# Joining the softmax parts of a dilated attention by exchanged log-sums, before the norm, in a two-layer decoder kernel

## Chip, core and metric

One core of one Trainium2 chip. The metric is device time of one execution of the whole kernel in microseconds (us), the median of several runs. The profile comes from one execution.

## What is computed

A decoder trunk on x (512 tokens, 1024 channels, f32): an RWKV-7 layer, a SwiGLU feed-forward, a dilated attention layer, a second feed-forward. The change is in the attention. Its core in the reference, for each of three groups (window, dilation) = (128, 1), (512, 4), (2048, 16):

```
q = rms_norm(qkv[:, :, g, 0], q_gain[g]) * scale      # 16 heads of 64
k = rms_norm(qkv[:, :, g, 1], k_gain[g])
logits = einsum(q_block, k_band) + bias               # keys t - j*dilation, banded
lse    = logsumexp(logits)
out_g  = exp(logits - lse) @ v
...
weights = softmax(stack(lse_g), axis=0)
o = sum_g(weights_g * out_g)
y = o.reshape(B, S, 1024) @ w_o
```

The kernel takes the three groups as two softmax parts: the near part (group 0, blocks of 128 neighbouring tokens with the block before), and the far part (groups 1 and 2 in one row of logits, tokens sorted by residue modulo 4).

## The kernel before

Everything lies transposed (channels on partitions, tokens along the free dimension). Weights come as 512 KB panels through two raw slots. A panel is split into a high and a low fp32r part, by ScalarE (`split_high`, line 1290) and VectorE (`split_low`, line 1722), two panels ahead of its use. A `product` is three fp32r matmuls of 128x512 for each of eight weight blocks; one output tile is 24 such matmuls.

The attention layer runs over eight head pairs. A pass `it` of the loop makes the nine tiles of pair `it` (query, key, value of three groups, i = 0 to 8) and weaves in the attention of the pair before, a = it - 1, in an order written out by hand for each engine:
- `projection_aux`: sum of squares of a query or key tile into bank 4 by two matmuls; ScalarE's Ln (1605) and Exp (1607) make the norm, VectorE applies it (2109, 2112). For a value tile, four transposes into bank 4 and a copy (1609). Squares are split by ScalarE and POOL first (1592, 1596, 2344).
- `logits`: four steps a pair (0 and 1 near, 2 and 3 far) into bank 2 + h for head h, at tiles 0 to 3. VectorE adds the bias and takes the maximum (2126), and negates it (2135).
- `exps` (1618, Ln at 1623) after tiles 2 and 4; `normalize` scales the probabilities by the inverse sums of their own part (2141 to 2152).
- `flip_probs`: transposes of probabilities (line 579) into bank 5, four groups for each head, at tiles 3 to 6, copied by ScalarE (1631); `attend` multiplies values with them at tiles 4 to 7, near into bank 6, far into bank 7.
- `lse_difference` at tile 7: 16 products with 128 columns into bank 4, which spread the difference of the log-sums over all tokens; sigmoid on ScalarE (1644, with two table loads); `combine` on VectorE (2160 to 2165): near - far, times the sigmoid, plus far; then copy and subtraction make the high and low parts of the result (1635, 2169).

Nearly all matmuls go through one helper at line 576, the transposes through 579. `fill_att` makes TensorE wait until a bank's use before was read, `att_read` makes an engine wait until it has been. SP issues the panels and, for each pair, the bias rows (line 565). `last_pair` weaves the attention of the eighth pair into the first tiles of the output projection (`heads(m, chunk)`, each three matmuls; chunk c needs the result of pair c).

## Time and profile before

| | |
|---|---|
| median of 3 runs | 1822.44 us (1822.4 to 1822.57) |
| profiled execution | 1821.82 us, its span 1820.0 us |
| TensorE busy | 1792.6 us, 98% |
| VectorE, ScalarE, POOL busy | 874.5, 768.8, 197.1 us |
| HBM | 89 GB/s over the span |

Busy times of TensorE are modelled ends and overlap, so starts are the better measure. An engine that is idle off the chain that ended last costs nothing.

### The profile page before, as it was taken

How to read it: one execution, taken by the hardware profiler on the slowest of the kernel's cores; microseconds unless marked ns; L12 is line 12 of the kernel's file. 1: busy time of each engine (PE TensorE's matmuls, PEld its weight loads, DVE VectorE, ACT ScalarE, POOL GpSimd, SP SyncE). 2: the span in 40 equal slices, each digit the busy share in tenths (PEclk: the TensorE clock that was granted, in tenths of full speed). 3: DMA queues.
4: the chain of work that ended last, by engine and by line, in shares of the span. 5: the costliest groups of instructions: out<-in, count | busy, mean ns of one | idle time of the engine just before them, and what ended most of it. 6: DMA issues, size and time to landing. Idle time of an engine off the chain costs nothing.

```text
span 1820.0 us, 36178 instructions
## 1 busy us (share of the span) xinstructions
PE 1792.6 (98%) x15618; PEld 1368.7 (75%) x15618; DVE 874.5 (48%) x1517; ACT 768.8 (42%) x1308; POOL 197.1 (11%) x172
## 2 busy tenths in 40 slices
PE   8999999999999999999999999999999999999999
PEld 3746666666478888888887887887887788888887
DVE  5824444454364444333455555555555544444322
ACT  6434444442252232222556656656657532323221
POOL 0033334432100000000111111111110000000000
PEclk9999999999999999999999999999999999999999
DMA  3321212121123323333232222222222123223332
GB/s 125 103 69 51 82 67 67 64 98 53 59 93 98 99 93 94 103 100 98 93 93 70 82 82 70 81 82 70 81 83 70 62 94 100 93 94 103 100 98 93
DMA packets 57541, 155.00 MB, mean 85 GB/s; under 512 B 5591, under 2 KB 22535, under 8 KB 57384
## 3 DMA queue, kind: packets, MB, share of 16 engines
q1 hardware_dynamic: 57288, 152.63, 26.0%
q8 instruction: 124, 2.03, 0.5%
q14 instruction: 33, 0.27, 0.0%
q10 hardware_dynamic: 96, 0.07, 0.0%
HBM read 150.51 MB, written 11.61 MB: 89 GB/s over the span
## 4 chain that ended last, share of the span: by engine, by line
PE 92%; ACT 4%; DVE 2%; issue 1%; DMA 1%; POOL 1%; ACTq 0%; DVEq 0%; POOLq 0%
PE bank L576 89%; PE bank L579 3%; ACT f L1618 2%; DVE f L2152 0%; DVE r L2024 0%; ACT f L1605 0%; ACT f L1631 0%; ACT r L1290 0%; ACT r L1596 0%; DMA f<-const 0%; DMA f<-stream 0%; ACT f L1592 0%; DVE r L1722 0%; DVE f L1733 0%; DVE f L1769 0%
## 5 line engine op out<-in xcount | busy, mean ns | idle before, releaser
L576 PE MATMUL bank<-r 128*128 128x512 f32 x5424 | 1255.6, 391 | 2.3 <-DVE r L2024 1.0
L576 PEld LDWEIGHTS bank<-r 128*128 128x128 f32 x5424 | 1012.0, 188 | 225.3 <-issue 10.8
L576 PE MATMUL bank<-f 64*64 64x64 f32 (+5 forms) x9762 | 503.5, 255 | 16.5 <-ACT f L1315 4.2
L1722 DVE TENSOR_TENSOR r<-f,r 128x1024 fp32r<-128x1024 f32 x222 | 274.8, 1238 | 392.4 <-ACT r L1290 392.4
L576 PEld LDWEIGHTS bank<-f 64*64 64x64 f32 (+3 forms) x9762 | 308.7, 140 | 200.6 <-issue 133.1
L1290 ACT ACTIVATE r<-f 128x1024 fp32r<-128x1024 f32 x222 | 232.5, 1048 | 147.4 <-PE bank L576 141.5
L2344 POOL TENSOR_TENSOR r<-f,r 128x512 fp32r<-128x512 f32 x48 | 62.2, 1295 | 839.1 <-ACT r L1596 839.1
L1575 ACT ACTIVATE r<-f 128x512 fp32r<-128x512 f32 x44 | 27.8, 632 | 215.6 <-DVE f L2063 215.6
L2093 DVE TENSOR_TENSOR f<-bank,f 128x512 f32<-128x512 f32 x72 | 56.2, 780 | 73.4 <-PE bank L576 70.1
L1572 ACT ACTIVATE f<-f 128x512 f32<-128x512 f32 x44 | 27.8, 632 | 110.5 <-DVE f L2053 110.5
L1605 ACT ACTIVATE f<-bank,f 128x512 f32<-128x512 f32 x48 | 32.9, 686 | 94.9 <-PE bank L576 94.9
L579 PE MATMUL bank<-f 128*128 128x128 f32 x432 | 63.9, 277 | 5.4 <-DVE f L2152 4.3
L2057 DVE TENSOR_TENSOR f<-bank,f 128x512 f32<-128x512 f32 x44 | 30.4, 691 | 76.5 <-PE bank L576 76.5
L1631 ACT ACTIVATE f<-bank 128x512 f32<-128x512 f32 (+1 forms) x64 | 36.2, 566 | 71.6 <-PE bank L579 71.4
L579 PEld LDWEIGHTS bank<-f 128*128 128x128 f32 x432 | 49.3, 140 | 21.9 <-ACT f L1631 7.8
L1618 ACT ACTIVATE f<-f 128x256 f32<-128x256 f32 (+1 forms) x128 | 61.4, 482 | 2.6 <-DVE f L2135 2.6
L1448 ACT ACTIVATE f<-bank 128x512 f32<-128x512 f32 (+1 forms) x40 | 23.8, 596 | 78.3 <-PE bank L576 78.3
L2109 DVE SCALAR_TENSOR_TENSOR f<-f 128x512 f32<-128x512 f32 x32 | 37.0, 1155 | 30.0 <-ACT f L1607 30.0
L1860 DVE TENSOR_TENSOR f<-bank,f 128x512 f32<-128x512 f32 x40 | 27.7, 691 | 46.9 <-PE bank L576 46.9
L1867 DVE COPY f<-bank 128x512 f32<-128x512 f32 (+1 forms) x40 | 27.7, 692 | 46.1 <-PE bank L576 46.0
L2053 DVE TENSOR_TENSOR f<-bank,f 128x512 f32<-128x512 f32 x44 | 30.4, 691 | 32.4 <-PE bank L576 27.4
L2126 DVE CUSTOM_DVE_ANT_0 f<-bank,f 128x256 f32<-128x256 f32 (+1 forms) x128 | 44.4, 402 | 1.9 <-PE bank L576 1.1
(109 smaller groups left out, 919.4 us busy)
## 6 DMA issues: line engine op xcount, KB each, us to landing
f<-stream SPq DMA_DIRECT2D x246, 512.0 KB, 3.5
bias_copies<-bias_rows SPq DMA_DIRECT2D x6, 1536.0 KB
f<-xT SPq DMA_DIRECT2D x16, 256.0 KB, 4.6
f<-lora_out SPq DMA_DIRECT2D x16, 128.0 KB, 6.4
f<-bias_copies SPq DMA_DIRECT2D x16, 128.0 KB, 3.2
f<-bias_copies SPq DMA_DIRECT2D x32, 64.0 KB, 2.9
outT<-f SPq DMA_DIRECT2D x8, 256.0 KB, 4.3
f<-const SPq DMA_DIRECT2D x1, 576.0 KB, 3.7
```

The lines of the kernel that those rows point to most:

```text
L576: return nc.tensor.matmul(out, lhsT, rhs, start=start, stop=stop, skip_group_check=True)
L579: return nc.tensor.transpose(out, in_, con(C_ID))
L1290: A(r(hi_at(q), 1024), f(O_RAW + p % RAW * 1024, 1024), ACT.Copy)\
L1605: free(A(f(O_QS), banks[4][:, :], ACT.Ln, bias=kol(K_EPS), scale=1.0 / HD), 4)
L1618: A(tile, tile, ACT.Exp, bias=f(sm + 8 + n, 1), accum_out=f(sm + 16 + n, 1))\
L1631: free(A(f(O_PT + n % N_PT * S, w), banks[5][:, 0:w], ACT.Copy), 5)
L1722: TT(r(lo_at(q), 1024), f(O_RAW + panel_of(q) % RAW * 1024, 1024), rf(hi_at(q), 1024), ALU.subtract).then_inc(s["w_lo"], 1)
L2053: TT(f(O_FT + i % 2 * S), bank_of(t)[:, :], f(O_RSTD), ALU.mult)\
L2093: TT(out, in0, in1, ALU.mult).then_inc(freed(t), 1)
L2109: STT(by_residue(to), bc(f(O_QR + n % 2 * S), (4, P), (1, 4)), gain, bc(f(O_QS), (4, P), (1, 4)), ALU.mult, ALU.mult).then_inc(s["qk_norm" ...
L2126: ins = V.tensor_tensor_reduce(out=f(O_P + h * 4 * S + n * 2 * P + first, w), in0=banks[b][:, e * 2 * P + first:(e + 1) * 2 * P], in1=f(O_ ...
L2344: TT(r(O_QL), f(O_QQ), rf(O_QH), ALU.subtract).then_inc(s["q_sq_lo"], 1)
```

## The change

- The near queries are written so that inside a block of 128 tokens they are sorted by residue modulo 4 (VectorE norm in four pieces), and the near bias rows come in the same order: four DMAs of 32 partitions in place of one, for each head.
- `exchange_lse` replaces `lse_difference`: right after tile 5, four products with a 128x128 selection matrix and 16 columns bring each row the log-sums of the other part. VectorE picks them, subtracts its own and clips (`other_lse`), ScalarE takes one Exp (`weights`), VectorE makes 1 / (own sum * (1 + exp(difference))) (`scales`). The probabilities are scaled with this (`normalize`), so both parts add up in bank 6 and nothing is combined afterwards. The far attends write bank 6 in four runs of 32 columns.
- `logits` runs two steps at tile 1 and two at tile 3, even ones into banks 2 and 3, odd ones into 5 and 7. On ScalarE the exponentials stand ahead of the norm of tiles 1 and 3.
- Transposes go to bank 5 for head 0 and 7 for head 1, both heads together, at tiles 6, 7, 8 and tile 0 of the next pass; attends at tile 8 and tile 1 of the next pass.
- `last_pair` has a new order. Near the kernel's start one small constant (4 columns) is loaded more, on which the first bias product waits.

The diff, cut to its core (removed code can be read in the kernel above):

```diff
--- before.py
+++ after.py
@@ -396,23 +397,24 @@
+        def logits_bank(h, pair):
+            return 5 + 2 * h if pair % 2 else 2 + h
...
         def att_step(b, name, hp):
             if b in (2, 3):
...
+                return 2 * hp + name[1] // 2
+            if b in (5, 7):
+                return 6 * hp + (name + 2 if isinstance(name, int) else name[1] // 2)
...
             if name == "lse":
-                return base(hp + 1) + (8 if hp < NHP - 1 else 1)
+                return base(hp + 1) + (6 if hp < NHP - 1 else 1)
...
-            return base(hp) + (name + 1 + (name == 7) if hp else name)
+            return base(hp) + (name + 1 + (name >= 5) if hp else name)
...
@@ -502,6 +504,7 @@
+                    sp.dma_start(f(O_SM + 80, 4), const[:, C_QUARTER:C_QUARTER + 4]).then_inc(s["oh_in"], 16)
@@ -557,8 +560,14 @@
                     if hp:
-                        att_read(sp, 2 + h, (h, 3), hp - 1)
-                    for g, at, width in ((0, 0, 2 * P), (1, 2 * P, P), (2, 3 * P, P)):
+                        for pair in (2, 3):
+                            att_read(sp, logits_bank(h, pair), (h, pair), hp - 1)
+                    for c in range(4):
+                        src = bass.AP(tensor=bias_copies.tensor, offset=(2 * hp + h) * P * 384 + P - 1 + 383 * c,
+                                      ap=[[4 * 383, 32], [1, 2 * P]])
+                        sp.dma_start(f(O_BIAS + h * S, 2 * P, 32 * c, 32 * c + 32), src).then_inc(s[f"bias_in{h}"], 16)
+                    for g, at, width in ((1, 2 * P, P), (2, 3 * P, P)):
@@ -1134,7 +1143,7 @@
                         for h in range(2):
-                            o = banks[2 + h][:, e * 2 * P:(e + 1) * 2 * P]
+                            o = banks[logits_bank(h, pair)][:, e * 2 * P:(e + 1) * 2 * P]
...
@@ -1148,44 +1157,42 @@
+            def flip_probs(hp, g):
+                for h in range(2):
+                    b = 5 + 2 * h
+                    fill_att(b, g, hp)
+                    pe.wait_ge(s[f"probs{h}"], 8 * hp + (4 if g < 2 else 8))
+                    for j, what in enumerate(GROUPS[g]):
+                        last = flip(banks[b][:, j * P:(j + 1) * P], f(block_of(h, what), P))
+                    last.then_inc(s["flipped"], 1)
             def attend(hp, g):
                 for h in range(2):
...
+                    att_read(pe, 5 + 2 * h, g, hp)
+                if g == 0:
+                    if hp:
+                        pe.wait_ge(s["att_lo"], hp)
+                    att_read(pe, 4, 2, hp)
                 if g == 2:
                     att_read(pe, 4, 8, hp)
-                if g == 0:
-                    att_read(pe, 4, 2, hp)
                 for j, (kind, q, e) in enumerate(GROUPS[g]):
...
+                    v = O_VT + hp % 2 * 3 * S + (q - 1 + e) * P if kind == "A" else O_VT + (hp % 2 * 3 + 1 + e) * S + q * P
                     for h in range(2):
                         lo, n = HD * h, flip_turn(hp, h, g)
-                        last = mm(banks[b][lo:lo + HD, q * P:(q + 1) * P], f(v + lo, HD),
-                                  f(O_PT + n % N_PT * S + j * P, P), g in (0, 2) and j == 0, False)
+                        o = banks[6][lo:lo + HD, :].rearrange("p (n c j) -> p n c j", n=4, c=4)
+                        last = mm(o[:, q, :, :] if kind == "A" else o[:, :, q, :], f(v + lo, HD),
+                                  f(O_PT + n % N_PT * S + j * P, P), g == j == 0, False)
                 last.then_inc(s["attended"], 1)
-            def lse_difference(hp):
+            def exchange_lse(hp):
                 fill_att(4, "lse", hp)
...
+                pe.wait_ge(s["lse"], hp + 1)
+                if hp == 0:
+                    pe.wait_ge(s["quarters"], 1)
+                for c in range(4):
+                    last = mm(banks[4][:, 16 * c:16 * (c + 1)], f(O_E4 + c * P, P), bc(f(O_SM + 32, 48), (40, 2), (1, 8)))
                 last.then_inc(s["lse_ps"], 1)
...
             for it in range(NHP):
...
                 for i in range(9):
...
@@ -1206,16 +1213,22 @@
                     if i == 0:
                         projection_aux(a, 8)
...
+                    if i == 0 and b >= 0:
+                        flip_probs(b, 3)
+                    if i in (1, 3):
+                        logits(a, i - 1)
                         logits(a, i)
...
+                    if i == 1 and b >= 0:
+                        attend(b, 2)
+                        attend(b, 3)
+                    if i == 5:
+                        exchange_lse(a)
+                    if i in (6, 7):
+                        flip_probs(a, i - 6)
+                    if i == 8:
+                        attend(a, 0)
+                        attend(a, 1)
+                        flip_probs(a, 2)
             def last_pair(a):
@@ -1225,38 +1238,36 @@
                 heads(0, 0)
                 projection_aux(a, 8)
+                flip_probs(a - 1, 3)
                 logits(a, 0)
+                attend(a - 1, 2)
                 heads(0, 1, 2)
+                attend(a - 1, 3)
                 logits(a, 1)
...
                 logits(a, 3)
...
+                heads(1, 1, 2, 3, 4, 5)
+                heads(2, 0, 1, 2, 3, 4)
+                exchange_lse(a)
+                heads(2, 5)
+                heads(3, 0, 1, 2, 3)
+                flip_probs(a, 0)
+                heads(3, 4)
+                flip_probs(a, 1)
+                heads(3, 5)
                 attend(a, 0)
...
+                flip_probs(a, 2)
+                heads(0, 6)
                 attend(a, 1)
...
+                flip_probs(a, 3)
                 attend(a, 2)
-                flip_probs(a, 1, 3)
-                heads(2, 4, 5)
+                heads(1, 6)
                 attend(a, 3)
...
+                heads(2, 6)
+                heads(3, 6)
                 for m in range(4):
                     heads(m, KC - 1)
@@ -1597,6 +1608,8 @@
             def projection_aux(hp, i):
...
+                if kind == 2 and hp >= 2:
+                    act.wait_ge(s["attended"], 4 * (hp - 2) + (4 if g else 2))
                 act.wait_ge(s["aux_ps"], 9 * hp + i + 1)
@@ -1627,78 +1640,62 @@
-                w = len(GROUPS[g]) * P
-                free(A(f(O_PT + n % N_PT * S, w), banks[5][:, 0:w], ACT.Copy), 5)
+                w, b = len(GROUPS[g]) * P, 5 + 2 * h
+                free(A(f(O_PT + n % N_PT * S, w), banks[b][:, 0:w], ACT.Copy), b)
+            def weights(hp):
+                act.wait_ge(s["ex_step"], 7 * hp + 6)
+                A(f(O_EX + 112, 16), f(O_EX + 112, 16), ACT.Exp).then_inc(s["ex_exp"], 1)
             def combine(hp):
-                att_read(act, 7, None, hp)
-                A(r(O_O + hp * S), f(O_DF), ACT.Copy).then_inc(s["att_hi"], 1)
+                act.wait_ge(s["attended"], 4 * (hp + 1))
+                A(r(O_O + hp * S).rearrange("p (n j c) -> p n j c", n=4, c=4),
+                  banks[6][:, :].rearrange("p (n c j) -> p n j c", n=4, c=4), ACT.Copy).then_inc(s["att_hi"], 1)
...
+            def keep_both(a, g):
+                for h in range(2):
+                    keep_flipped(a, h, g)
             for it in range(NHP):
...
                 for i in range(9):
...
+                    split_high(p_of(T_QKV + 9 * it + i) + LEAD)
+                    if a >= 0 and i in (2, 4):
+                        for h in range(2):
+                            exps(a, h, i // 2 - 1)
                     if i:
                         projection_aux(it, i - 1)
-                    if a >= 0 and 3 <= i <= 6:
-                        keep_flipped(a, 1, i - 3)
+                    elif a >= 0:
+                        projection_aux(a, 8)
+                    if i == 0 and b >= 0:
+                        keep_both(b, 3)
+                    if a >= 0 and i in (6, 7):
+                        keep_both(a, i - 6)
...
+                    if i == 2 and b >= 0:
+                        combine(b)
+                    if i == 5:
+                        weights(a)
+                    if i == 8:
+                        keep_both(a, 2)
             def last_pair(a):
                 projection_aux(a, 8)
+                keep_both(a - 1, 3)
                 split_high(PAN_WO1 + 3)
+                combine(a - 1)
                 exps(a, 0, 0)
                 exps(a, 1, 0)
                 split_high(PAN_WO1 + 4)
-                keep_flipped(a, 0, 0)
                 exps(a, 0, 1)
-                keep_flipped(a, 1, 0)
                 exps(a, 1, 1)
...
+                weights(a)
+                for g in range(4):
+                    keep_both(a, g)
                 combine(a)
...
@@ -2102,21 +2099,28 @@
+                        for h in range(2):
+                            dve.wait_ge(s[f"logits{h}"], 4 * (hp - 1))
...
+                    elif kind == 0:
+                        for c in range(4):
+                            part = lambda off: bc(f(off + c, S - 3), (P, 4), (4, 32))
+                            last = STT(bc(f(to + 32 * c, S - 96), (P, 4), (1, 32)), part(O_QR + n % 2 * S), gain,
+                                       part(O_QS), ALU.mult, ALU.mult)
+                        last.then_inc(s["qk_norm"], 1)
@@ -2131,68 +2135,91 @@
             def negate_max(hp, h, half):
...
-                att_read(dve, 2 + h, (h, 2 * half + 1), hp)
+                for pair in (2 * half, 2 * half + 1):
+                    att_read(dve, logits_bank(h, pair), (h, pair), hp)
                 TS(f(sm + 8, 4), f(sm, 4), -1.0, None, ALU.mult).then_inc(s[f"neg_max{h}"], 1)
+            def both_heads(off, n=8):
+                return bc(f(off, 40 + n), (40, 2), (1, n))
+            def total(hp):
+                for h in range(2):
+                    dve.wait_ge(s[f"log{h}"], 2 * hp + 2)
+                TT(both_heads(O_SM + 32), both_heads(O_SM + 32), both_heads(O_SM), ALU.add).then_inc(s["lse"], 1)
+            def other_lse(hp):
+                def step(ins, n):
+                    ins.then_inc(s["ex_step"], 1)
+                    dve.wait_ge(s["ex_step"], 7 * hp + n)
+                dve.wait_ge(s["lse_ps"], hp + 1)
+                att_free(TT(bc(f(O_EX, 64), (4, 16), (1, 4)), banks[4][:, 0:64].rearrange("p (u n) -> p u n", n=4),
+                            bc(f(O_SM + 80, 4), (0, 16), (1, 4)), ALU.mult), 4)
+                att_read(dve, 4, "lse", hp)
+                step(TT(bc(f(O_EX + 64, 32), (2, 16), (1, 2)), bc(f(O_EX, 62), (4, 16), (1, 2)),
+                        bc(f(O_EX + 2, 62), (4, 16), (1, 2)), ALU.add), 1)
+                step(TT(f(O_EX + 96, 16), bc(f(O_EX + 64, 31), (2, 16)), bc(f(O_EX + 65, 31), (2, 16)), ALU.add), 2)
+                for half in range(2):
+                    step(TT(bc(f(O_EX + 112 + 4 * half, 12), (8, 2), (1, 4)),
+                            bc(f(O_EX + 96 + 1 - half, 15), (2, 2), (4, 4)),
+                            both_heads(O_SM + 32 + 4 * half, 4), ALU.subtract), 3 + half)
+                step(TS(f(O_EX + 112, 16), f(O_EX + 112, 16), 80.0, None, ALU.min), 5)
+                TS(f(O_EX + 112, 16), f(O_EX + 112, 16), -80.0, None, ALU.max).then_inc(s["ex_step"], 1)
+            def scales(hp):
+                dve.wait_ge(s["ex_exp"], hp + 1)
+                STT(both_heads(O_SM + 24), bc(f(O_EX + 112, 16), (8, 2), (1, 8)), kol(K_ONE), both_heads(O_SM + 16),
+                    ALU.add, ALU.mult).then_inc(s["ex_step"], 1)
+                dve.wait_ge(s["ex_step"], 7 * hp + 7)
+                V.reciprocal(both_heads(O_SM + 24), both_heads(O_SM + 24)).then_inc(s["inv_sum"], 1)
             def normalize(hp, h, half):
...
+                dve.wait_ge(s["inv_sum"], hp + 1)
                 for n in range(4):
                     first = P if n == half == 0 else 0
                     tile = f(O_P + h * 4 * S + (4 * half + n) * 2 * P + first, 2 * P - first)
                     TS(tile, tile, f(sm + 24 + n, 1), None, ALU.mult).then_inc(s[f"probs{h}"], 1)
...
             def combine_low(hp):
+                natural = lambda ap: ap.rearrange("p (n j c) -> p n j c", n=4, c=4)
                 dve.wait_ge(s["att_hi"], hp + 1)
-                TT(r(O_O + (KC + hp) * S), f(O_DF), rf(O_O + hp * S), ALU.subtract).then_inc(s["att_lo"], 1)
+                TT(natural(r(O_O + (KC + hp) * S)), banks[6][:, :].rearrange("p (n c j) -> p n j c", n=4, c=4),
+                   natural(rf(O_O + hp * S)), ALU.subtract).then_inc(s["att_lo"], 1)
...
+            V.tensor_copy(bc(f(O_E4), (P, 4), (32, 4), (1, 32)), bc(con(C_ID), (32, 4), (0, 4), (1, 32)))\
+                .then_inc(s["quarters"], 1)
...
             for it in range(NHP):
...
                 for i in range(9):
+                    if a >= 0 and i == 5:
+                        total(a)
...
+                    if i in (1, 3):
                         for h in range(2):
+                            biased(a, h, i - 1)
                             biased(a, h, i)
...
+                            negate_max(a, h, i // 2)
+                    if i == 3 and b >= 0:
+                        combine_low(b)
+                    if i == 5:
+                        other_lse(a)
+                        scales(a)
+                    if i in (5, 6):
                         for h in range(2):
-                            normalize(a, h, i // 2 - 1)
+                            normalize(a, h, i - 5)
             def last_pair(a):
@@ -2206,18 +2233,18 @@
                 negate_max(a, 0, 0)
                 negate_max(a, 1, 0)
                 split_low(PAN_WO1 + 3)
+                combine_low(a - 1)
                 both(2)
-                normalize(a, 0, 0)
                 both(3)
                 negate_max(a, 0, 1)
                 negate_max(a, 1, 1)
...
                 split_low(PAN_WO1 + 4)
...
+                total(a)
+                other_lse(a)
+                scales(a)
+                for half in range(2):
+                    for h in range(2):
+                        normalize(a, h, half)
                 combine_low(a)
...
```

## Rows read from the trace of the kernel before

**Rows 1.** The page: busy time of each engine, and the chain that ended last.
```profile
PE 1792.6 (98%) x15618; PEld 1368.7 (75%) x15618; DVE 874.5 (48%) x1517; ACT 768.8 (42%) x1308; POOL 197.1 (11%) x172
...
PE 92%; ACT 4%; DVE 2%; issue 1%; DMA 1%; POOL 1%; ACTq 0%; DVEq 0%; POOLq 0%
```

**Rows 2.** Windows, one pass: length, busy us (count) of PE, PEld, DVE, ACT, POOL, clock.
```profile
1059.50:1127.90 68.40, 67.77 (x413) 55.01 (x412) 37.46 (x89) 41.94 (x85) 7.77 (x6) 1.00 0.24 79
```

**Rows 3.** Waits of TensorE, 923 to 1401 us (total, times, longest).
```profile
PE bank L579 <- DVE f L2152: 4.3, 7, 0.6
```

**Rows 4.** Timeline of TensorE in one pass: start, length, what, how many.
```profile
1066.43 1.13 PE L576 MATMUL bank<-f 64*128 64x256 f32 x8
...
1080.29 1.03 PE L579 MATMUL bank<-f 128*128 128x128 f32 x8
1081.25 1.16 PE L576 MATMUL bank<-f 64*128 64x128 f32 x16
1082.35 0.65 PE L579 MATMUL bank<-f 128*128 128x128 f32 x4
1082.76 6.19 PE L576 MATMUL bank<-r 128*128 128x512 f32 x26
1088.78 0.49 PE L579 MATMUL bank<-f 128*128 128x128 f32 x3
1089.20 1.09 PE L576 MATMUL bank<-f 128*64 128x128 f32 x16
1090.22 0.55 PE L579 MATMUL bank<-f 128*128 128x128 f32 x3
...
1098.59 0.63 PE L579 MATMUL bank<-f 128*128 128x128 f32 x4 [0.63 <-DVE f L2152]
...
1113.04 2.84 PE L576 MATMUL bank<-f 128*64 128x128 f32 x48
1115.81 11.63 PE L576 MATMUL bank<-r 128*128 128x512 f32 x50
1127.28 0.60 PE L579 MATMUL bank<-f 128*128 128x128 f32 x4
```

**Rows 5.** The last of 26 stream matmuls, then ScalarE's timeline after it.
```profile
1066.12 0.39 PE L576 MATMUL bank<-r 128*128 128x512 f32 x1
...
1066.54 0.69 ACT L1605 ACTIVATE f<-bank,f 128x512 f32<-128x512 f32 x1 [3.06 <-PE bank L576]
1067.26 0.63 ACT L1607 ACTIVATE f<-f 128x512 f32<-128x512 f32 x1
```

**Rows 6.** Timeline of VectorE: combining, small steps, norm by residue, scaling.
```profile
1059.73 0.68 DVE L2160 TENSOR_TENSOR f<-f,bank 128x512 f32<-128x512 f32 x1
1060.44 0.69 DVE L2163 TENSOR_TENSOR f<-f 128x512 f32<-128x512 f32 x1
...
1069.97 0.64 DVE L2135 TENSOR_SCALAR f<-f 128x4 f32<-128x4 f32 x2
...
1079.41 0.18 DVE L2141 RECIPROCAL f<-f 128x4 f32<-128x4 f32 x1 [0.71 <-ACT f L1618]
...
1097.31 1.14 DVE L2152 TENSOR_SCALAR f<-f 128x256 f32<-128x256 f32 x4
...
1114.53 1.15 DVE L2109 SCALAR_TENSOR_TENSOR f<-f 128x512 f32<-128x512 f32 x1 [1.14 <-ACT f L1607]
```

**Rows 7.** Bias loads on SP: min/median/max ns of one issue.
```profile
L565 SPq DMA_DIRECT2D f<-bias_copies x48: 319/432/1643, 885.8 to 1362.1; - x48
```

**Rows 8.** Timeline of TensorE in the last pair: first small piece, the two waits, the end.
```profile
1396.25 0.63 PE L579 MATMUL bank<-f 128*128 128x128 f32 x4
...
1411.34 0.55 PE L579 MATMUL bank<-f 128*128 128x128 f32 x3 [0.21 <-ACT f L1631]
...
1416.31 0.66 PE L579 MATMUL bank<-f 128*128 128x128 f32 x4 [0.77 <-ACT f L1631]
...
1424.80 11.41 PE L576 MATMUL bank<-r 128*128 128x512 f32 x49
```

More of the change, by code:

```diff
@@ L80 @@
 C_OH = C_RESET + 512
-N_CONST = C_OH + 3 * 384
+C_QUARTER = C_OH + 3 * 384
+N_CONST = C_QUARTER + 4
 def shape_constants():
@@ L214 @@
 O_BIAS = O_VR + S
-O_OA = O_BIAS + 2 * S
-O_DF = O_OA + S
-O_DW = O_DF + S
-assert O_DW + S <= O_B
+O_EX = O_BIAS + 2 * S
+O_E4 = O_EX + S
+assert O_E4 + S <= O_B
 O_O = O_HD
@@ L1128, in logits @@
                 for h in range(2):
-                    fill_att(2 + h, (h, pair), hp)
+                    fill_att(logits_bank(h, pair), (h, pair), hp)
                 pe.wait_ge(s["qk_norm"], 6 * hp + (2 if pair < 2 else 6))
@@ L1149, in block_of @@
                 return O_P + h * 4 * S + (n + (4 if kind == "B" else 0)) * 2 * P + e * P
-            def flip_probs(hp, h, g):
-                fill_att(5, (h, g), hp)
-                pe.wait_ge(s[f"probs{h}"], 8 * hp + (4 if g < 2 else 8))
-                for j, what in enumerate(GROUPS[g]):
-                    last = flip(banks[5][:, j * P:(j + 1) * P], f(block_of(h, what), P))
-                last.then_inc(s["flipped"], 1)
+            def flip_probs(hp, g):
[6 more added lines that the diff above has]
+                    last.then_inc(s["flipped"], 1)
@@ L1158, in attend @@
             def attend(hp, g):
                 for h in range(2):
-                    att_read(pe, 5, (h, g), hp)
-                if g in (0, 2):
-                    fill_att(6 if g == 0 else 7, None, hp)
+                    att_read(pe, 5 + 2 * h, g, hp)
[3 more added lines that the diff above has]
+                    att_read(pe, 4, 2, hp)
                 if g == 2:
                     att_read(pe, 4, 8, hp)
-                if g == 0:
-                    att_read(pe, 4, 2, hp)
@@ L1176, in attend @@
                 last.then_inc(s["attended"], 1)
-            def lse_difference(hp):
+            def exchange_lse(hp):
                 fill_att(4, "lse", hp)
-                for h in range(2):
-                    pe.wait_ge(s[f"lse{h}"], 2 * (hp + 1))
-                for n in range(2 * NT):
-                    for h in range(2):
-                        lo = HD * h
-                        o = banks[4][lo:lo + HD, n * P:(n + 1) * P] if n < NT else \
-                            banks[4][lo:lo + HD, n - NT:S:4]
-                        last = mm(o, bc(f(O_SM + 40 * h + 32 + n, 1), (0, HD)), con(C_ID), n == 0, False)
+                pe.wait_ge(s["lse"], hp + 1)
[3 more added lines that the diff above has]
+                    last = mm(banks[4][:, 16 * c:16 * (c + 1)], f(O_E4 + c * P, P), bc(f(O_SM + 32, 48), (40, 2), (1, 8)))
@@ L1195, in _ @@
             for it in range(NHP):
-                a = it - 1
+                a, b = it - 1, it - 2
                 for i in range(9):
@@ L1662, in _ @@
                     if i:
                         projection_aux(it, i - 1)
-                    if a >= 0 and 3 <= i <= 6:
-                        keep_flipped(a, 1, i - 3)
+                    elif a >= 0:
[4 more added lines that the diff above has]
+                        keep_both(a, i - 6)
                     squares(it, i)
@@ L2115, in biased @@
             def biased(hp, h, pair):
-                b = 2 + h
+                b = logits_bank(h, pair)
                 dve.wait_ge(s[f"logits{h}"], 4 * hp + pair + 1)
-                dve.wait_ge(s[f"bias_in{h}"], 48 * (hp + 1))
+                dve.wait_ge(s[f"bias_in{h}"], 96 * (hp + 1))
                 if hp:
@@ L2137, in normalize @@
+            def scales(hp):
[4 more added lines that the diff above has]
+                V.reciprocal(both_heads(O_SM + 24), both_heads(O_SM + 24)).then_inc(s["inv_sum"], 1)
             def normalize(hp, h, half):
                 sm = O_SM + 40 * h + 4 * half
-                dve.wait_ge(s[f"exp{h}"], 8 * hp + 4 * half + 4)
@@ L2141, in normalize @@
-                V.reciprocal(f(sm + 24, 4), f(sm + 16, 4)).then_inc(s["inv_sum"], 1)
-                inv = 4 * hp + 2 * half + h + 1
-                dve.wait_ge(s[f"log{h}"], 2 * hp + half + 1)
-                if half:
-                    TT(f(sm + 32, 4), f(sm + 8, 4), f(sm + 32, 4), ALU.subtract).then_inc(s[f"lse{h}"], 1)
-                else:
-                    TT(f(sm + 32, 4), f(sm, 4), f(sm + 32, 4), ALU.add).then_inc(s[f"lse{h}"], 1)
-                dve.wait_ge(s["inv_sum"], inv)
+                dve.wait_ge(s["inv_sum"], hp + 1)
@@ L2182, in _ @@
                         continue
-                    if i == 0 and a:
-                        combine(a - 1)
-                    if i < 4:
+                    if i in (1, 3):
                         for h in range(2):
+                            biased(a, h, i - 1)
                             biased(a, h, i)
-                        if i % 2:
-                            for h in range(2):
-                                negate_max(a, h, i // 2)
-                    if i == 0 and a:
-                        combine_low(a - 1)
-                    if i in (2, 4):
+                            negate_max(a, h, i // 2)
[5 more added lines that the diff above has]
+                    if i in (5, 6):
                         for h in range(2):
-                            normalize(a, h, i // 2 - 1)
+                            normalize(a, h, i - 5)
             def last_pair(a):
```

98 lines of the change are left out of this document (4 added, 94 removed).

## The prediction

> **What bounds the kernel now.** I read the page first: TensorE is busy 98% of the span and the chain that ended last is 92% TensorE [rows 1]. So only what TensorE executes, or waits for, can move the time. Next the windows: one pass of the attention loop (nine projection tiles of one head pair, with the attention of the pair before woven in) is 68.4 us long [rows 2], seven such passes follow each other, and the last pair is woven into the output projection. Its clock stays at 1.00, so nothing of the clock enters the sum. In the list of waits TensorE waits in the seven passes for one thing, a VectorE scaling of probabilities, 0.6 us each time [rows 3]. ScalarE (41.9 us of 68.4) and VectorE (37.5) have room, but in places only.
>
> In the timeline of one pass [rows 4] I subtract starts from starts, since the printed ends overlap. The pass falls into eight pieces of the 228 stream matmuls (the products, and the sums of squares made with them), 53.0 us, and eight pieces of small work, the first at 1066.43 and the last at 1127.28: 1.07, 1.10, 2.47, 1.75, 2.41, 2.40, 2.77 and 1.38 us, together 15.35. That is 68.35, the whole pass. I price the parts from the same rows. Sixteen attend matmuls alone take 1.02, sixteen with 32 log-sum matmuls 2.77: so 0.0547 each, 1.75 for the log-sums, and about 0.145 for leaving such a piece. Eight transposes before an attend piece take 0.96, three 0.42: 0.108 each and 0.1 for the change; four before the stream take 0.41 (1082.35 to 1082.76), no extra. Logits of one step: 1.38 less four transposes, 0.53, is 0.85 for the first, then 1.07, 1.10 and 1.10 (1081.25 to 1082.35), each with some 0.1 for leaving. An unbroken piece of 50 stream matmuls takes 11.47 (1115.81 to 1127.28), one of 26 takes 6.02 (1082.76 to 1088.78): 24 more are 5.45, 0.227 each, so 26 should be 5.90 and a break costs 0.12.
>
> **The change on TensorE, per pass.** After it, small work stands in seven places:
> - tile 0: 4 transposes of the value tile and 8 of probabilities: 1.25
> - tile 1: two logits steps and 32 attend matmuls: 0.85 + 1.07 - 0.1 + 1.75 + 0.145 = 3.7
> - tile 3: 4 value transposes, two logits steps: 0.52 + 1.10 + 1.10 - 0.1 = 2.6
> - tile 5: the exchange, and a new wait (below)
> - tile 6: 12 transposes 1.25; tile 7: 6 transposes 0.6; tile 8: 28 attend matmuls and 8 transposes, 1.68 + 0.85 = 2.5.
>
> The exchange is 4 products with 16 columns, thus 8 instructions (each f32 product is two: the 8 products of the first attend group stand as 16). No row has 16 columns on full weights. From below: 128 columns take 0.109, so 16 take 0.014, 0.1 in all. From above: each as long as a whole transpose, 0.109, 0.9 in all. I take 0.6, nearer the upper end, since the weights to be loaded are the transposes' own size; with leaving the piece 0.7.
>
> **The new wait.** The exchange writes bank 4, directly after the sums of squares of tile 4 were put there. It must wait until ScalarE's Ln of line 1605 has read them. Before, 16 attends stood between. Ln starts 0.42 us after the start of the last of those matmuls and takes 0.69 [rows 5]; TensorE resumes 0.14 after a releaser's end (the scalings from 1097.31 end at 1098.45, it starts at 1098.59) [rows 4, 6]. It would have gone on 0.31 after that start (1066.12 to 1066.43). So 0.42 + 0.69 + 0.14 - 0.31 = 0.94, say 0.93 us of wait per pass. Behind it on TensorE stand the next product and everything after.
>
> Sum of small work: 1.25 + 3.7 + 2.6 + 0.7 + 0.93 + 1.25 + 0.6 + 2.5 = 13.5. The old wait is already within the 15.35. Stream: one break less, 0.1. Net per pass 15.35 - 13.5 + 0.1 = 1.95; I take 1.9, for mode changes (logits to attends) that no row shows side by side. Seven passes: 13.3.
>
> **Does the long chain fit?** The exchange must now reach the probabilities before the first transposes, one tile later. Count from the end of tile 4's sums: Ln and Exp end at 1.4, VectorE's norm by residue (1.15) at 2.6 [rows 5, 6]. Behind it on VectorE are the exchange's seven steps. A small one lasts 0.18, and a dependent one starts 0.03 after the end before it (1060.41 to 1060.44) [rows 6]: with the wider first one 1.4, to 4.0. ScalarE's Exp of 16 columns, taken as about as short, 0.25; addition and reciprocal 0.4: 4.7. Scaling four blocks takes 1.07 per head: 5.8 and 6.9. TensorE gets there after wait 0.8, exchange 0.7, product 5.6 and value transposes 0.45: 7.65, and 8.2 for the second head. So the cover is there, with 1.3 to 1.8 us left, and the old wait of 0.6 goes and nothing takes its place in tile 6. What is queued behind ScalarE's wait for VectorE (`weights`) is the split of a weight panel two tiles ahead: some 3 us later, used 8 us later. The next nearest: ScalarE's two copies of transposes (0.6 each) stand ahead of the squares of tile 7; POOL then needs 1.3, and I find 1.0 us left before TensorE asks for them.
>
> **Moved or removed beside TensorE, costed at nothing.** VectorE's three combining steps and ScalarE's near copy, sigmoid and two table loads go [rows 5, 6]. The exponentials (4 x 0.5 us and a Ln for each head, 4.5 a half) now stand ahead of Ln/Exp of tiles 1 and 3 on ScalarE: by my count they end 1.1 us before tile 1's sums and 0.15 after tile 3's, which have a whole tile until anybody needs them. VectorE's query norm of the first group becomes four pieces (0.75 to about 1.2), logits use it a pass later. SP issues 12 instead of 6 bias loads per pair, at 0.43 each, 2.6 us more ahead of one weight panel [rows 7], and waits for the last biased bank about 1.5 us longer. A panel is split two tiles (14 us) before its use, which hides it. The extra small load at the start stands ahead of weight panels by one issue, 0 to 0.4 us.
>
> A rule of the Trainium skill (PSUM — Partial Sum Buffer, Specifications) speaks against the change: it says of the 8-byte cachelines that any non-contiguous access pattern "slows matmuls significantly", and the far groups now write bank 6 in four runs of 32 with gaps. The trace disagrees for a stricter pattern: half of the 32 log-sum matmuls write every fourth column, and all 48 together fit one price of 0.0547 us [rows 4].
>
> **The last pair.** Its small pieces take 14.05 us now (ten of them between 1396.25 and 1424.80) [rows 8]; built as above they are 15.1, since the previous pair's third and fourth attends and last transposes (2.6 us) come in and 1.05 of the log-sums goes. The two waits of 0.21 and 0.77 there and their slow restarts go: 1.1. New ones: 0.35 for the second head's probabilities, 0.1 for a bank, 0.1 to 0.2 at the end, where the joined result of the last pair now has two products (1.4 us) as cover for copy 0.65 and subtraction 0.69, instead of ten. Net 0.5 more. In exchange the first pass is without a pair behind it: 2.6 less.
>
> **Sum.** 13.3 + 2.6 - 0.5 = 15.4 us. The profiled execution took 1821.82 us (span 1820.0); the median of the runs is 0.6 above it. 1822.4 - 15.4 = 1807.0; I say 1807.2 with the start's load.
>
> **Rivals.**
> 1. The chain is late (slower side). If each of some nine dependent steps between exchange and scaling costs 0.57, near the 0.64 that two small negations behind a reduction take together [rows 6], instead of 0.2, the chain is 3.3 us longer. From 1.3 us on it decides; 2.0 us per pass come onto TensorE, 14, and some 3.3 in the last pair: 1824.5. Against it: those stand behind a reduction, the reciprocal and the subtraction of the combining do not and take 0.18 and 0.69 + 0.03. 7%.
> 2. The strided write costs. If the 32 far attends took double, 1.75 for eight pairs is 14: 1821.2. The Trainium skill's rule above would give this; the rows speak against. 7%, with everything else that would end within 0.2%.
> 3. The change doesn't do what its last words say: merging logits in four banks saves nothing, as new changes of shape cost what old ones did. Of the 1.9 per pass, 1.15 is the exchange, 0.8 the old wait, -0.93 the new; 0.9 is merging. Without it 6.3 less gain: 1813.5. 10%.
> 4. ScalarE's copies ahead of the squares hold TensorE at tile 7: if 2 us late instead of 1 early, 1 us per pass: 1814. 9%.
> 5. More than forecast: the exchange hides at the lower bound (0.5 x 8) and no mode change costs: 1802. 9%.
>
> The forecast has 58% (1804 to 1811). A measurement of this kernel can tell about 0.2% (3.6 us): faster by more 86%, within 7%, slower 7%. The range reaches over forecast and rivals 3 and 4, and a little of 5: 1803 to 1817.
>
> **What would show it.** Pass 66.4 us instead of 68.3. TensorE's wait for VectorE's scaling gone from the list of waits, one for Ln of line 1605's successor there with 0.9 us seven times, before a piece of 8 matmuls with 16 columns. That piece 0.3 to 0.9. A piece of 32 attends near 1.75 (double would be rival 2). If TensorE waits for the scaling in tile 6, rival 1; for POOL or the squares in tile 8, rival 4. The forecast is wrong if the pass is above 67.5 or below 65.5.

## The result and the profile after

The changed kernel took 1804.83 us, median of 4 runs (1803.7 to 1806.13), against 1822.51 for the kernel before on the same chip (1822.4 to 1826.07): ratio 0.9901, 95% interval 0.9886 to 0.9917. That is 17.7 us, or 1.0%, faster. The prediction said 1807.2, range 1803 to 1817, faster with 86%.

The profiled execution took 1806.13 us, its span is 1804.3, 15.7 less than the span before. The busy times on its page:

```profile
PE 1775.9 (98%) x15426; PEld 1362.0 (75%) x15426; DVE 881.7 (49%) x1534; ACT 741.6 (41%) x1285; POOL 198.4 (11%) x172
```

TensorE is still the bound, busy 98%, but with 192 instructions and 16.7 us of busy time less than in [rows 1]. The chain in order of time (start, length, what) shows where the time went:

```profile
520.83 366.81 PE bank L585 x1614
...
1023.53 0.69 ACT f L1618
...
1089.84 0.69 ACT f L1618
...
1445.69 355.45 PE bank L585 x1565
```

From the first of these rows (in the first feed-forward) to the last (the start of the second one's stream) is 924.86 us. The same chain of before has 520.30 for the first and 1461.37 for the last, 941.07 us: 16.2 less. Up to the first row the profile after is 0.5 later, and after the last both run 355.5. Where the first of the seven passes begins, it is still 0.5 later (923.50 against 922.99), so all of the gain lies in the attention layer. One pass, from Ln to Ln (line 1618 after, 1605 before), is 66.31 us, 1089.84 - 1023.53, instead of 68.35 (68.4 in the window of [rows 2]).

The timeline of TensorE over one pass, tile 0 to tile 8 (start, length, what, how many, idle time before and what ended it):

```profile
1052.77 1.47 PE L588 MATMUL bank<-f 128*128 128x128 f32 x12
1054.00 6.17 PE L585 MATMUL bank<-r 128*128 128x512 f32 x26
1060.10 3.69 PE L585 MATMUL bank<-f 64*128 64x128 f32 x48
1063.71 11.63 PE L585 MATMUL bank<-r 128*128 128x512 f32 x50
1075.18 0.60 PE L588 MATMUL bank<-f 128*128 128x128 f32 x4
1075.71 2.06 PE L585 MATMUL bank<-f 64*128 64x128 f32 x32
1077.70 12.10 PE L585 MATMUL bank<-r 128*128 128x512 f32 x52
1090.58 1.06 PE L585 MATMUL bank<-f 128*128 128x16 f32 x8 [0.78 <-ACT f L1618]
1091.49 5.73 PE L585 MATMUL bank<-r 128*128 128x512 f32 x24
1097.06 1.47 PE L588 MATMUL bank<-f 128*128 128x128 f32 x12
1098.29 6.18 PE L585 MATMUL bank<-r 128*128 128x512 f32 x26
1104.31 0.82 PE L588 MATMUL bank<-f 128*128 128x128 f32 x6
1104.88 6.17 PE L585 MATMUL bank<-r 128*128 128x512 f32 x26
1110.98 1.75 PE L585 MATMUL bank<-f 128*64 128x128 f32 x28
1112.66 1.09 PE L588 MATMUL bank<-f 128*128 128x128 f32 x8
1113.51 5.73 PE L585 MATMUL bank<-r 128*128 128x512 f32 x24
```

Seven pieces of small work, as forecast: from the start of each to the start of the stream behind it they take 1.23, 3.61, 2.52, 0.91 (the exchange), 1.23, 0.57 and 2.53 us, and the exchange is preceded by a wait. The list of TensorE's waits over the attention layer (total, times, longest), which answers to [rows 3]:

```profile
PE bank L585 <- ACT f L1618: 5.4, 7, 0.8
PE bank L588 <- DVE f L2186: 0.4, 1, 0.4
```

The wait for scaled probabilities in every pass is gone, and the one for ScalarE's Ln is there, seven times 0.78. Rival 1 would have shown line 2186 here seven times; it stands there once, in the last pair, where 0.35 was forecast. Rival 4 would have shown a wait for POOL or for the squares of tile 7, and none is in the list. VectorE's chain in the same pass:

```profile
1091.22 1.14 DVE L2107 SCALAR_TENSOR_TENSOR f<-f 128x512 f32<-128x512 f32 x1 [0.79 <-ACT f L1620]
1092.21 0.21 DVE L2158 TENSOR_TENSOR f<-bank,f 128x64 f32<-128x64 f32 x1
...
1093.96 0.23 DVE L2174 SCALAR_TENSOR_TENSOR f<-f 128x16 f32<-128x16 f32 x1 [0.28 <-ACT f L1648]
...
1094.51 2.06 DVE L2186 TENSOR_SCALAR f<-f 128x128 f32<-128x128 f32 x8
```

The exchange's steps start at 1092.21, after the norm of line 2107, and the probabilities of both heads are scaled at 1096.57. TensorE's first transposes of them come after the four of the value tile, at about 1097.5. Read from these rows, the chain fits with some 1.4 to 1.8 us left; the experiment with 13 more steps below finds 1.2.

### The profile page after: what moved, and what is told of

It reads as the page before. It is cut to its first block, busy times and chain, and to the rows that moved or that the text cites. A ratio compares the mean times of both kernels' runs of the same rounds, so it can differ in the third digit from the quotient of the medians.

```text
span 1804.3 us, 35872 instructions
## 1 busy us (share of the span) xinstructions
PE 1775.9 (98%) x15426; PEld 1362.0 (75%) x15426; DVE 881.7 (49%) x1534; ACT 741.6 (41%) x1285; POOL 198.4 (11%) x172
## 4 chain that ended last, share of the span: by engine, by line
PE 95%; DVE 2%; ACT 1%; issue 1%; DMA 1%; POOL 1%; SPq 0%; ACTq 0%; DVEq 0%; POOLq 0%
PE bank L585 92%; PE bank L588 3%; DVE r L2021 0%; ACT f L1618 0%; ACT r L1301 0%; DMA f<-xT 0%; DMA f<-const 0%; DMA f<-stream 0%; DVE r L1719 0%; DVE f L1730 0%; DVE f L1766 0%; DVE r L1775 0%; DVE f L2033 0%; DVE f L2186 0%; POOL f L2290 0%
## 5 line engine op out<-in xcount | busy, mean ns | idle before, releaser
L585 PE MATMUL bank<-f 64*64 64x64 f32 (+7 forms) x9570 | 490.4, 254 | 22.4 <-ACT f L1618 5.4
L1719 DVE TENSOR_TENSOR r<-f,r 128x1024 fp32r<-128x1024 f32 x222 | 280.3, 1263 | 376.5 <-ACT r L1301 376.5
L585 PEld LDWEIGHTS bank<-f 64*64 64x64 f32 (+3 forms) x9570 | 302.2, 140 | 205.9 <-issue 127.9
L588 PE MATMUL bank<-f 128*128 128x128 f32 x432 | 57.8, 275 | 0.4 <-DVE f L2186 0.4
L1459 ACT ACTIVATE f<-bank 128x512 f32<-128x512 f32 (+1 forms) x40 | 23.8, 596 | 77.9 <-PE bank L585 77.9
L2130 DVE CUSTOM_DVE_ANT_0 f<-bank,f 128x256 f32<-128x256 f32 (+1 forms) x128 | 44.9, 402 | 12.6 <-PE bank L585 11.7
L1622 ACT ACTIVATE f<-bank 128x512 f32<-128x512 f32 x24 | 14.3, 597 | 79.3 <-PE bank L588 79.3
```

The lines of the kernel that those rows point to most:

```text
L585: return nc.tensor.matmul(out, lhsT, rhs, start=start, stop=stop, skip_group_check=True)
L588: return nc.tensor.transpose(out, in_, con(C_ID))
L1719: TT(r(lo_at(q), 1024), f(O_RAW + panel_of(q) % RAW * 1024, 1024), rf(hi_at(q), 1024), ALU.subtract).then_inc(s["w_lo"], 1)
L2130: ins = V.tensor_tensor_reduce(out=f(O_P + h * 4 * S + n * 2 * P + first, w), in0=banks[b][:, e * 2 * P + first:(e + 1) * 2 * P], in1=f(O_ ...
```

## The experiments

In the following, "stretch" is the time between the two long TensorE pieces of the chain shown above (924.86 us after, 941.07 before). It is used because the time up to the first one differs between profiles of equal code: it is at 520.83 us in the profile after and at 515.62 in a second profile of the same kernel, whose stretch is 924.90. The readings of each version come from one profile of it.

### The new wait taken away: the exchange in another bank

```diff
+        def lse_bank(hp):
+            return 2 if hp < NHP - 1 else 4
...
-                    last = mm(banks[4][:, 16 * c:16 * (c + 1)], ...
+                    last = mm(bank[:, 16 * c:16 * (c + 1)], ...
```

(with the turns of banks 2 and 4, and VectorE's read, changed to match)

> The changed kernel with the exchange of the first seven pairs in bank 2, which is free by then, instead of bank 4; the last pair as it was. My theory: the 0.78 us in which TensorE waits for ScalarE's Ln of tile 4's sums is a pure loss, so the piece after the last sum starts 0.2 instead of 1.17 us after it, a pass takes 66.31 - 0.94 = 65.4 us and the span is 6.6 us shorter than the changed kernel's 1804.3. Rival: VectorE's chain from exchange to scaled probabilities is anchored at the same Ln, so TensorE only waits 0.9 us later, at the transposes of tile 6, and the pass stays at 66.3.

Stretch 917.67 us, 7.2 less; a pass 65.28. The exchange stands in the stream with no idle time ahead of it:

```profile
1082.71 0.96 PE L590 MATMUL bank<-f 128*128 128x16 f32 x8
1083.52 5.75 PE L590 MATMUL bank<-r 128*128 128x512 f32 x24
```

No wait for line 1618's Ln is left, and none came at the transposes. So the wait was a pure loss of 1.03 us a pass (0.94 expected): 0.78 idle and some 0.25 around it. Of these, 0.10 lie in the piece itself, which takes 0.81 without a pause ahead of it (1082.71 to 1083.52) instead of 0.91. The rival falls.

### Logits apart

```diff
-                    if i in (1, 3):
-                        logits(a, i - 1)
+                    if i < 4:
                         logits(a, i)
```

> The changed kernel with the four logits steps issued apart, at tiles 0, 1, 2 and 3, still in four banks; VectorE's order is unchanged. My theory: merging them saves changes of shape; apart, the pass has one break more in the stream and three more changes, 0.17 + 0.10 + 0.09 + 0.10 + 0.13 = 0.6 us, so 66.9 us a pass and 4.2 us in all. Rival (merging saves nothing, what changed is only which bank): the pass stays at 66.3.

Stretch 930.59 us, 5.7 more; a pass is 67.13, 0.82 more. The steps at tiles 0, 1 and 2 of such a pass:

```profile
1053.12 0.93 PE L585 MATMUL bank<-f 64*128 64x128 f32 x8
1053.98 6.19 PE L585 MATMUL bank<-r 128*128 128x512 f32 x26
1060.10 3.03 PE L585 MATMUL bank<-f 64*128 64x256 f32 x40
...
1069.17 1.16 PE L585 MATMUL bank<-f 64*128 64x128 f32 x16
```

The first step costs 0.86 here, and the stream is broken again at 1069.17. Merging is thus worth 0.82 us a pass, more than the 0.6 expected here, and rival 3 of the prediction (0.9 of the gain doesn't come) falls. Counting the changes of shape gives the right sign and about the size; it does not explain 0.2 of the 0.82.

### The far part written without gaps

```diff
-                        last = mm(o[:, q, :, :] if kind == "A" else o[:, :, q, :], f(v + lo, HD),
+                        last = mm(o[:, q, :, :], f(v + lo, HD),
```

> The changed kernel with the far attends written to 128 neighbouring columns of bank 6 instead of four runs of 32 (the parts are thus added in the wrong order of tokens; the work is the same). My theory: the write pattern costs nothing, pass and span stay within 0.3 us. Rival (the Trainium skill, PSUM — Partial Sum Buffer, Specifications: patterns that are not contiguous slow matmuls): the 32 far attends of a pair, 0.77 to 0.92 us a group of 16 now, get clearly shorter, up to 0.9 us a pass.

The output of this version is wrong, since its far parts land on the wrong tokens. Stretch 924.89 us, a difference of 0.03; the piece with 16 logits and 32 attend matmuls in it has the same length to 0.01 us:

```profile
1054.99 3.69 PE L585 MATMUL bank<-f 64*128 64x128 f32 x48
1058.61 5.73 PE L585 MATMUL bank<-r 128*128 128x512 f32 x24
```

TensorE's output in runs of 32 f32 columns with gaps costs nothing here. The sentence of the Trainium skill (PSUM — Partial Sum Buffer, Specifications) does not hold for this write, and rival 2 falls.

### The exponentials behind the norm

```diff
-                    if a >= 0 and i in (2, 4):
-                        for h in range(2):
-                            exps(a, h, i // 2 - 1)
                     if i:
                         projection_aux(it, i - 1)
...
                     squares(it, i)
                     if a < 0:
                         continue
+                    if i in (2, 4):
+                        for h in range(2):
+                            exps(a, h, i // 2 - 1)
```

> The changed kernel with ScalarE's exponentials behind the norm and the squares of their tile, as before the change. In the prediction I costed their place at nothing. Seen from the trace after, I now expect that it costs: the second half would run from about 1086.4 to 1091 instead of ending at 1083.8, so the Ln for which TensorE waits at the exchange starts about 2.2 us later, the wait grows from 0.8 to 3 us and a pass takes 68.5 us, the span 15 us more. Rival (place costs nothing): 66.3 a pass.

Stretch 960.11 us, 35 more than after and 19 more than before; the passes take 71.4 to 71.8, only the first 70.5. The direction was as expected, the size more than twice that: the waits are 3.3 to 3.6 us (2.7 in the first pass), against 3 expected, and what follows them is slow.

```profile
1171.83 1.89 PE L585 MATMUL bank<-f 128*128 128x16 f32 x8 [3.63 <-ACT f L1618]
1173.56 7.52 PE L585 MATMUL bank<-r 128*128 128x512 f32 x24
1180.92 1.47 PE L588 MATMUL bank<-f 128*128 128x128 f32 x12
```

The eight instructions take 1.73 us instead of 0.91, and the 24 of the stream 7.36 instead of 5.57 (1091.49 to 1097.06). That is 2.6 us, beside 2.85 of longer wait in this pass: 66.31 + 2.6 + 2.85 = 71.8. The windows (length, TensorE's busy time, granted clock, DMA share, GB/s) show why:

```profile
1154.00:1168.00 14.00, 14.00 (x86) 1.00 0.41 114
...
1171.80:1173.50 1.70, 1.67 (x8) 0.50 0.08 14
1173.50:1176.00 2.50, 2.50 (x8) 0.50 0.60 200
1176.00:1178.00 2.00, 2.00 (x8) 0.66 0.00 0
```

The granted clock is 1.00 before the pause and 0.50, the lower of its two levels (1.2 GHz), after it, until about 1177.4. So the place of the exponentials, which the prediction costed at nothing, is what makes the exchange right after tile 5 pay: they have to be out of ScalarE's way before the Ln that TensorE waits for.

### How much cover the chain has

```diff
+                for k in range(13):
+                    TS(f(O_EX + 112, 16), f(O_EX + 112, 16), -80.0, None, ALU.max).then_inc(s["pad"], 1)
+                    dve.wait_ge(s["pad"], KC + 13 * hp + k + 1)
```

> The changed kernel with 13 more dependent VectorE steps (a clip repeated, no change of values) between exchange and scaling: 13 x 0.21 = 2.7 us. In the trace after, the first head's scaling ends some 1.8 us and the second's 1.4 us ahead of its transposes. My theory (a cover, then microsecond for microsecond): TensorE comes to wait 1.0 for the first head and 0.5 more for the second in tile 6, pass 67.8 us; in the last pair, where nothing is left, 2.7: some 13 us in all. Rival 1 of the prediction (each step costs 0.57): 7.4 us more chain, 6 us a pass, 45 us. Rival (chain not on the path at all): 66.3 a pass.

Stretch 939.57 us, 14.7 more; a pass 67.83. VectorE's 13 steps and TensorE's transposes in one pass:

```profile
1093.56 2.69 DVE L2170 TENSOR_SCALAR f<-f 128x16 f32<-128x16 f32 x13
...
1098.52 0.63 PE L588 MATMUL bank<-f 128*128 128x128 f32 x4 [0.80 <-DVE f L2189]
1099.50 0.63 PE L588 MATMUL bank<-f 128*128 128x128 f32 x4 [0.36 <-DVE f L2189]
```

A dependent small step costs 0.21 us (2.69 / 13), not 0.57. The 2.7 us of delay come out as 1.52 a pass: so 1.2 us of it were covered, near the 1.3 that the prediction named as the point from which the chain decides. The mechanism of rival 1 is real, its price isn't. In the last pair the delay costs 4.0 us instead of 2.7. There the pause is 2.79 us, and the windows show the low clock after it, as above:

```profile
1413.70 0.83 PE L588 MATMUL bank<-f 128*128 128x128 f32 x4 [2.79 <-DVE f L2189]
...
1414.00:1416.00 2.00, 1.85 (x9) 0.50 0.00 0
1416.00:1418.00 2.00, 2.00 (x10) 0.65 0.00 0
```

### A pause between those

The same, with 19 steps.

> The changed kernel with 19 more dependent VectorE steps in the chain, 4.0 us. With 13 steps (2.7 us) TensorE waited 0.80 and 0.36 us and its clock stayed at 1.00; after a pause of 2.8 us in the last pair, and of 3.6 us with the exponentials last, the granted clock showed 0.50 for some microseconds. Theory A (only waits): a pause of 2.1 and one of 0.36, pass 67.83 + 1.27 = 69.1 us. Theory B (a pause of 2.1 us already brings the lower clock): the stream after it runs at half speed for some 2 to 4 us, pass 70 to 72 us, and the clock of the pass under 1.00.

Stretch 956.53 us. Six passes in order (length, TensorE busy, clock, DMA share, GB/s):

```profile
981.27:1051.97 70.70, 67.51 (x389) 0.98 0.25 75
1051.97:1121.06 69.09, 65.90 (x389) 1.00 0.25 77
1121.06:1191.73 70.67, 67.48 (x390) 0.98 0.25 75
1191.73:1260.79 69.06, 65.88 (x389) 1.00 0.26 77
1260.79:1329.86 69.07, 65.88 (x390) 1.00 0.26 77
1329.86:1400.54 70.68, 67.50 (x390) 0.98 0.25 75
```

Both theories hold in turn. With the same pause of 2.05 us in each of these six, the clock fell after it in three, which take 70.7, and stayed in three, which take 69.07, as theory A says to 0.1 us. The seventh such pause stands ahead of these windows, in the first pass (2.04 us, TensorE resumes at 963.40), and there the clock fell too: 0.50 from 964 to 966. So it fell after four of seven equal pauses, and cost 1.3 us in the first pass and 1.6 in the others. The last pair has a pause of 4.05 us, after which it fell as well. Why one pass and not the next is open.

### The width of the exchange

```diff
-                    last = mm(banks[4][:, 16 * c:16 * (c + 1)], f(O_E4 + c * P, P), bc(f(O_SM + 32, 48), (40, 2), (1, 8)))
+                    last = mm(banks[4][:, 64 * c:64 * (c + 1)], f(O_E4 + c * P, P), bc(f(O_SM + 32, 48), (0, 4), (40, 2), (1, 8)))
```

(with VectorE's read changed to match)

> The changed kernel with each of the four exchange products four times as wide (64 columns, the same sixteen repeated; VectorE reads the first sixteen). In the trace after the eight instructions follow each other every 0.112 us, which I had put at 0.6 for all and which is the price of a transpose with 128 columns. My theory: full 128x128 f32 weights set this price, not columns, so with 64 columns the piece still takes 0.91 us and a pass 66.3. Rival (a column price below 128, and a start of its own for each): the piece grows by 0.1 us or more.

Stretch 924.90 us, and the piece again 0.91 long:

```profile
1087.08 1.10 PE L585 MATMUL bank<-f 128*128 128x64 f32 x8 [0.78 <-ACT f L1618]
1087.99 5.73 PE L585 MATMUL bank<-r 128*128 128x512 f32 x24
```

Four times the columns cost nothing. So an f32 matmul on full weights costs the same at 16 and at 64 columns: 0.11 us here, behind a pause, and 0.10 in the last pair, where no pause stands ahead (8 in 0.80 us with 64 columns, in 0.81 with 16). Twelve transposes with 128 columns take 1.23 us, 0.10 each, too. That it is the load of the weights which sets this price is argued, not shown: the log-sum products had half the weights and cost half, 0.0547, with 128 columns, but no run changed the weights alone.

### The removed products by themselves

```diff
-                for n in range(2 * NT):
+                for n in range(2 * NT - 1, 2 * NT):
```

(with the output's columns changed to match)

> The kernel before, with only the last of the eight log-sum steps made (2 of 16 products: the output's weights are wrong). This measures the removed work by itself: 28 of 32 instructions at 0.0547 are 1.53 us a pass, so 68.36 - 1.53 = 66.8 us, 12.3 us in all with the last pair. Rival: the products were hidden behind ScalarE's Ln or another wait, then less; the wait of 0.63 for scaled probabilities stays in both.

This version leaves out 14 of the 16 products and so gives a wrong output. Stretch 930.39 us against 941.07 before, 10.7 less, where 12.3 were expected; a pass is 66.84, 1.52 less, as worked out. But 7 x 1.52 is already 10.6: in the last pair nothing was gained. Its waits in the list (total, times, longest):

```profile
PE bank L579 <- DVE f L2151: 4.3, 7, 0.6
PE bank L579 <- ACT f L1630: 1.3, 3, 0.8
PE bank L579 <- DVE f L2092: 1.2, 1, 1.2
```

In the loop the log-sum products were on the path with their full price, in the last pair they filled time in which TensorE would otherwise have waited: its waits for ScalarE's copies are 1.3 us there instead of 1.0 before, and one of 1.2 for VectorE's value tile (line 2092) is new.

### A version faster than both

The exchange in bank 2 as above, and in `last_pair` two products moved up by one place: one more stands ahead of the first group of transposes, still one between the first two groups, and none right behind the second:

```diff
-                heads(3, 0, 1, 2, 3)
+                heads(3, 0, 1, 2, 3, 4)
                 flip_probs(a, 0)
-                heads(3, 4)
+                heads(3, 5)
                 flip_probs(a, 1)
-                heads(3, 5)
```

> The exchange in bank 2 for seven pairs, and in the last pair one more product ahead of the first transposes of probabilities (and one fewer between them and the second). Theory: passes of 65.28 as in the run before with that bank, 7.2 us less in all; the product ahead covers the waits of some 0.2 and 0.35 for scaled probabilities there, 0.3 to 0.6 us less: 7.6 us under the changed kernel on the same chip. Rival: the copies of transposes are then late for the third group and take the 0.5 back.

Beside it on the same chip the changed kernel once more:

> The changed kernel once more, as the measure for the next one on the same chip. The three profiles of it and its near variants differ by up to 5 us before the second layer begins and by nothing after it, so I expect the median within 1800 to 1806, passes of 66.31 and the last pair as before.

The changed kernel took 1803.13 us (1801.0 to 1803.99, ratio 0.9909, interval 0.9892 to 0.9925), this version 1798.1 (1797.11 to 1799.62, ratio 0.9880, interval 0.9865 to 0.9895), the kernel before 1819.9. Stretch 916.99, 7.9 less than the changed kernel's, as forecast (7.6); the medians are only 5.0 apart. In the two profiles the part before the stretch is 4.0 us longer in this version (519.64 against 515.62), which is within what equal code shows there; the other runs of the medians have no profile. No wait is left in the attention layer but one of 0.2 us at its end. The rival, late copies, did not come.

## Why the prediction was right

- **The bound.** TensorE's own time and waits decide: 16.2 us less in the stretch. The pieces and waits of TensorE account for all of it; ScalarE was relieved by 27 us, and no part of the gain is left over for that.
- **The sum per pass.** Forecast 1.9 less, measured 2.04. Of the pieces, forecast and measured: tile 0 1.25 and 1.23; tile 1 3.7 and 3.61; tile 3 2.6 and 2.52; tile 6 1.25 and 1.23; tile 7 0.6 and 0.57; tile 8 2.5 and 2.53. The mode change from logits to attends, for which I had taken 0.05 off, costs nothing extra. With the exchange at 0.91 the seven are 12.6, just the forecast without the wait, because what the exchange took more the others took less. So the sum is closer than its terms, and this is in part luck. The 0.1 by which the pass is better than the sum lies in the stream, which is 0.2 shorter instead of 0.1.
- **The exchange** was mis-sized: 0.6 and 0.1 for leaving it forecast, 0.91 measured. Of this, 0.10 comes with the pause ahead of it, as it takes 0.81 in another bank, so its own price is 0.10 an instruction, near the upper bound of the prediction. The width has no part in it. Rival 5's lower bound for it falls.
- **The new wait** stands where it was put, behind Ln, seven times; 0.78 idle. It costs 1.03 us, of which 0.10 is inside the exchange's piece, so 0.93 is left, the forecast.
- **The old wait** of 0.63 is gone and nothing took its place; the cover of the chain was 1.2 us in the experiment, 1.3 to 1.8 in the prediction.
- **The removed log-sums** are worth 1.52 us for 28 of 32 instructions, as priced, in the passes. In the last pair I counted them as a gain too; alone they are none there.
- **First pass and last pair.** The first of the seven passes, from the transposes of one value tile to the next, is 63.56 us instead of 68.20, 4.6 shorter: 2.0 as in each of the others, 2.75 for the missing pair behind it (forecast 2.6), less 0.15, by which the first pass before was already shorter than its fellows. What is left for the last pair is 0.7 longer instead of 0.5. So 6 x 2.04 + 4.6 - 0.7 = 16.2, against the forecast 15.4.
- **Costed at nothing**: the place of the exponentials. In the changed kernel it costs nothing, as said, but the prediction did not see how much rests on it: behind the norm, the wait would grow to 3.3 to 3.6 us and the gain turn into a loss.
- **Start.** The 0.5 us by which the profile after is later there is within what profiles of equal code differ, so the small load's price can't be told.

The medians give 17.7 us, the two profiles 15.7: the profiled execution after was 1.3 us above its median, the one before 0.7 below. As the stretch and what follows it repeat to 0.1 us in profiles of equal code, these 2 us probably lie in the part before the stretch, which no sum of the prediction covers. The median is 2.4 us under the forecast: 0.8 of this are terms of the sum, and the rest is probably scatter there.

## What to carry to other kernels

Where one engine is busy 98%, count its instructions by the distance of their starts, price a change of shape as an item of its own (0.1 to 0.2 us here) and merge small work into fewer pieces. When work is moved directly behind something that another engine must read, look at which buffer it writes: another free bank was worth 7 us here. A pause in the middle of dense work can cost more than its length, 1.8 times here (2.05 us of pause and 1.6 of slow work), as the clock may fall after it.

## What the runs showed of the hardware

- TensorE's granted clock stayed at 1.00 after pauses of 0.8 us, fell to 0.50 with every pause of 2.7 to 4.1 us, and with pauses of 2.05 us fell four times in seven. It was back at 1.00 some 4 to 6 us after the restart, and where this was worked out the fall cost 1.3 to 2.6 us.
- An f32 matmul with 128x128 weights takes 0.10 to 0.11 us whether it has 16, 64 or 128 columns.
- f32 output in four runs of 32 columns is as fast as 128 neighbouring ones, to 0.01 us in a piece of 3.6.
